# Modulation units placed singly, two groups of them behind the second norm, values turned two units later, and the residual loaded in four parts

## The reference

```python
mod = silu(c) @ w_ada + b_ada                    # 2048 x 12288, one row
sh1, sc1, g1, sh2, sc2, g2 = split(mod, 6)
h = rms_norm(x, g) * (1 + sc1) + sh1
u, q, k, v, ga, gb = split(h @ w_in)             # ga, gb: 2048 wide, the others 1024
y_ssm = s5_branch(u)                             # scan, gelu, then y * sigmoid(y @ w_glu)
y_att = attention(q, k, v)                       # 8 heads of 128
merged = sigmoid(ga) * (y_ssm @ w_proj_ssm) + sigmoid(gb) * (y_att @ w_proj_attn)
x = x + g1 * (merged @ w_out)
h2 = rms_norm(x, g') * (1 + sc2) + sh2           # the second norm
x = x + g2 * (square(relu(h2 @ w_ff1)) @ w_ff2)
x = rms_norm(x, g'')
# the second block: conv and gated recurrence, 32-head windowed attention, w_out_2, MLP; it is not touched
```

## Time and profile before

| | us |
|---|---|
| median of 3 runs | 3233.09 (3228.68 to 3240.85) |
| the profiled execution, its own time | 3230.05 |
| its span, first to last instruction | 3228.7 |
| PE busy in it | 3064.6 (95%) |
| DVE busy | 2135.8 (66%) |
| ACT busy | 1376.7 (43%) |
| mean granted clock of PE | 0.979 of full speed |

### The profile page before, as it was taken

The page is one execution under the profiler, slowest core; times in us unless marked ns, Lnnn a source line. Parts: engine busy times, 40 slices in busy tenths (PEclk is TensorE's granted clock), DMA queues, the critical chain, the costliest instruction groups (busy, mean ns, idle before and its releaser), DMA issues.

```text
span 3228.7 us, 48855 instructions
## 1 busy us (share of the span) xinstructions
PE 3064.6 (95%) x20283; PEld 2762.3 (86%) x20283; DVE 2135.8 (66%) x2568; ACT 1376.7 (43%) x1682; POOL 307.3 (10%) x255
## 2 busy tenths in 40 slices
PE   5799988998899999999998999999999999999998
PEld 1588878898888888888998999999999888888887
DVE  6689996677777554655787776666455755555555
ACT  2233323333353443434455564544444544444343
POOL 4547650000000000000000000000000100000000
PEclk8899999999999999999999999999999999999999
DMA  8855558867767666566555555445555556565664
GB/s 302 276 173 164 164 174 276 278 229 254 254 198 271 189 194 191 186 197 188 177 158 170 170 176 164 147 151 161 177 189 170 178 188 186 194 192 191 189 190 155
DMA packets 311483, 632.08 MB, mean 196 GB/s; under 512 B 30096, under 2 KB 34816, under 8 KB 310624
## 3 DMA queue, kind: packets, MB, share of 16 engines
q1 hardware_dynamic: 298496, 618.74, 59.4%
q10 hardware_dynamic: 11904, 5.61, 0.6%
q0 software_dynamic: 864, 4.60, 0.5%
HBM read 624.66 MB, written 4.21 MB: 195 GB/s over the span
## 4 chain that ended last, share of the span: by engine, by line
PE 77%; DVE 11%; DMA 7%; ACT 2%; issue 2%; ACTq 1%; SPq 0%; DVEq 0%
PE PS L918 13%; PE PS L905 12%; PE PS L906 11%; PE PS L907 11%; PE PS L922 7%; PE PS L934 6%; PE PS L936 6%; PE PS L935 6%; DVE wlo L1743 3%; DMA raw<-in_w_in 2%; ACT whi L2257 2%; DVE aacc L1732 2%; DMA raw<-in_w_ada 1%; DMA raw<-in_w_proj_attn 1%; DMA raw<-in_w_out 1%
## 5 line engine op out<-in xcount | busy, mean ns | idle before, releaser
L1743 DVE TENSOR_TENSOR wlo<-raw,whi 128x1024 fp32r<-128x1024 f32 x983 | 1244.4, 1270 | 920.9 <-ACT whi L2257 919.5
L2257 ACT ACTIVATE whi<-raw 128x1024 fp32r<-128x1024 f32 x983 | 1036.0, 1058 | 1386.7 <-PE PS L907 503.6
L905 PE MATMUL PS<-R,whi 128*128 128x256 f32 x4160 | 1209.5, 291 | 57.0 <-DVE wlo L1743 38.2
L906 PE MATMUL PS<-R,whi 128*128 128x256 f32 x4160 | 1189.4, 286 | 0.0
L907 PE MATMUL PS<-R,wlo 128*128 128x256 f32 x4160 | 1189.0, 286 | 0.0
L905 PEld LDWEIGHTS PS<-R,whi 128*128 128x128 f32 x4160 | 810.5, 195 | 99.4 <-issue 47.0
L906 PEld LDWEIGHTS PS<-R,whi 128*128 128x128 f32 x4160 | 811.0, 195 | 0.8 <-issue 0.7
L907 PEld LDWEIGHTS PS<-R,wlo 128*128 128x128 f32 x4160 | 810.2, 195 | 0.0
L918 PE MATMUL PS<-R,whi 128*128 128x512 f32 x1920 | 484.7, 395 | 14.7 <-DVE R L1660 8.6
L918 PEld LDWEIGHTS PS<-R,whi 128*128 128x128 f32 x1920 | 348.0, 190 | 78.6 <-issue 15.4
L934 PE MATMUL PS<-whi,R 128*128 128x512 f32 x896 | 350.1, 391 | 1.6 <-issue 0.9
(11 more groups left out here) (356 smaller groups left out, 1833.8 us busy)
## 6 DMA issues: line engine op xcount, KB each, us to landing
raw<-in_w_in SPq DMA_DIRECT2D x295, 512.0 KB, 4.1
raw<-in_w_ff SPq DMA_DIRECT2D x256, 512.0 KB, 4.0
raw<-in_w_ada SPq DMA_DIRECT2D x175, 512.0 KB, 4.8
raw<-in_w_mlp_up SPq DMA_DIRECT2D x128, 512.0 KB, 4.1
raw<-in_w_mlp_down SPq DMA_DIRECT2D x128, 512.0 KB, 3.9
raw<-in_w_out SPq DMA_DIRECT2D x64, 512.0 KB, 4.3
raw<-in_w_rnn_proj SPq DMA_DIRECT2D x32, 512.0 KB, 3.6
raw<-in_w_attn_proj SPq DMA_DIRECT2D x32, 512.0 KB, 3.7
```

The source lines that it names most:

```text
L905: pe.matmul(o, whi[:, s, c:c + P], x.operand.hi(k), start=first, stop=False, skip_group_check=True)
L906: pe.matmul(o, whi[:, s, c:c + P], x.operand.lo(k), start=False, stop=False, skip_group_check=True)
L1743: v.tensor_tensor(wlo[:, i % SPN, :], words(j), whi[:, i % SPN, :].bitcast(F32), ALU.subtract).then_inc(lo_done, 1)
L2257: a.activation(whi[:, i % SPN, :], words(j), ACT.Copy).then_inc(hi_done, 1)
```

## The change

- The planner's table gets other points, and at most one modulation unit follows a weight unit (two where four or more are late), where the old loop placed all that were late. By the new table groups 8 and 9 lie mostly behind unit 210 and end at unit 300.
- `turn_v` starts two units after the end of the v panel on PE; ACT's `turned_v` lets three turns pass first.
- The residual comes in four transfers of 512 KB, each with its own semaphore: quarter 0 after four heads and unit 137 (`unit_done` 138), quarter 2 after unit 145, quarter 1 after eight heads and unit 155, quarter 3 after unit 165. `rope_loads` stand behind them on POOL. DVE's residual of panel p waits for quarter p.
- `norm2` is started one unit earlier on ACT and DVE, ahead of the preparation of unit 203.

```diff
-ADAP = ((8, 0), (78, 16), (128, 62), (193, 107), (207, 107), (236, 128))
+ADAP = ((8, 0), (78, 16), (185, 96), (207, 96), (300, 128))
...
-        while extra and n >= resume and 128 - len(extra) < int(np.interp(n, xs_, ys_)):
+        late = int(np.interp(n, xs_, ys_)) - 128 + len(extra)
+        for e in range(min(1 if late < 4 else 2, late) if n >= resume else 0):
             units.append(extra.pop(0))
             if len(extra) % 16 == 0:
                 closes.append(close_at(n - LOOK + 1 + LAG))
                 resume = closes[-1][0] + LOOK + 1
+                break
...
-            if n in (end_of["v", 0], end_of["v", 1]):
-                new.append(turn_v(0 if n == end_of["v", 0] else 1))
+            for i in range(2):
+                if n == end_of["v", i] + 2:
+                    new.append(turn_v(i))
...
             if done is evac_v["res1"]:
-                v.wait_ge(x2_in, 16)
+                v.wait_ge(x2_in[p], 16)
...
-            if n == end_of["w_out", 3] + 1:
+            if n == end_of["w_out", 3]:
                 new.append(norm2())
...
         def turned_v(g):
+            for i in range(3):
+                yield
             for i in range(2):
                 a.wait_ge(v_turned, 2 * g + i + 1)
...
         def second_loads():
-            g.wait_ge(ya_ready, 8)
+
             g.wait_ge(x_saved, 16)
-            g.dma_start(fv(XR, 4096), scr_x).then_inc(x2_in, 16)
+            for p, heads, n in ((0, 4, 138), (2, 4, 146), (1, 8, 156), (3, 8, 166)):
+                g.wait_ge(ya_ready, heads)
+                g.wait_ge(unit_done, n)
+                g.dma_start(fv(XR + 1024 * p, 1024), scr_x[:, 1024 * p:1024 * p + 1024]).then_inc(x2_in[p], 16)
```

More of the change, by code:

```diff
@@ L300, in program @@
     acc_done, row_done = sem("acc_done"), sem("row_done")
-    c_in, small_in, x_in, hot_in, bc_in, bias_in, x2_in, rope_in = (sem(n) for n in (
-        "c_in", "small_in", "x_in", "hot_in", "bc_in", "bias_in", "x2_in", "rope_in"))
+    c_in, small_in, x_in, hot_in, bc_in, bias_in, rope_in = (sem(n) for n in (
+        "c_in", "small_in", "x_in", "hot_in", "bc_in", "bias_in", "rope_in"))
+    x2_in = [sem(f"x2_in{p}") for p in range(4)]
     x_saved, bias_saved, out_saved = sem("x_saved"), sem("bias_saved"), sem("out_saved")
@@ L2507, in side @@
                 bias_loads()
-            if n == end_of["pa", 3]:
+            if n == end_of["v", 1]:
                 second_loads()
```

## The result

The changed kernel took 3208.31 us (median of 4 runs, 3205.73 to 3209.66) against 3232.86 us of the kernel before beside it: 24.6 us less by the medians. The ratio over the runs is 0.9913, 95% interval 0.9899 to 0.9927, which is 24 to 33 us less. The forecast was 3189, in a range of 3170 to 3215: the direction and the range hold, the gain by the medians is a little over half of the 42.5 us of the sum, and 3208 lies nearer to the two rivals at 3211 and 3212 than to the forecast.

A forecast was written before the change was run, and what follows sets the result against it. PE, busy 95% of the span, bounds the kernel; only its idle and slow-clock time, mostly from late weight feed between 459 and 1031 us, can go. Terms sum to 42.5 us: 3230.05 − 42.5 = 3187.5, for a median 3189; range 3170 to 3215.

The forecast's parts named there:

- the two rivals at 3211 and 3212: 3211: only the three single waits count, 21.5 us, chance 0.12; 3212: units 152 to 186 at 2.3 us a unit, 0.14.
- the waits for `wlo` before 640 us: Sign of being right: PE's waits for these weights before 640 us come to under 4 us in all.
- the feed waits in units 152 to 186: Sign of being right: PE waits 10 to 20 us for weights in these units, more than before the change.
- nothing new is late: Units 104 to 127: turning v two units later removes waits of 6.45 and 4.8 us and delays nothing else.
- Bank 7 is used by nobody else meanwhile: At the later turn of v: no other work needs this PSUM bank, so the delay adds no wait.
- 4.5 us given: Units 138 to 151: loading the residual in quarters removes the 5.3 us wait around unit 152; saved 4.5.
- 0.8 us given to the norm: Units 187 to 199: starting the second norm earlier saves 0.8 us, within bounds of 0 to 1.2.
- units 84 to 103, 20 given: Weight feed without bursts of modulation units, at 1.8 us a unit, saves 20 us, or 13 at 2.0.
- the dense stretch, −4.6 given: Units 152 to 186: 64.7 units at 1.94 us each take 125.5 us, 4.6 lost; bounds 4.4 won, 8.5 lost.
- the rival's 2.3: Units 152 to 186: at 2.3 us a unit they take 149 us, 23 worse than the sum, total 3212; chance 0.14.
- behind unit 208, 4.4 given: Units 208 to 239: 4.35 us of PE idle time goes; with about 1 lost later, 3.4 saved.
- The two closes are moved, not changed: From 931 us: closes of two modulation groups come later, after unit 255, at unchanged cost.

The follow-up runs named there:

- e2: Changed kernel with the values turned at once, as before the change: 3206.11 us, ratio 0.9922 to the kernel before.
- e12: Changed kernel with a flatter planner table, ACT's panel-end rounding and squares and DVE's dependent steps one unit later, and values turned at once: 3188.94 us, ratio 0.9867.
- e1: Changed kernel with the old planner (old table, old loop), the other three parts kept: 3227.01 us, ratio 0.9987 to the kernel before.
- e3: Changed kernel with the residual loaded whole once the eighth head is done: 3213.18 us, ratio 0.9940 to the kernel before.
- e4: Changed kernel with norm2 started at unit 200 again: 3207.73 us, ratio 0.9923 to the kernel before.
- e5: Changed kernel loading 256 KB in place of 512 for each modulation unit of groups 2 to 9: 3207.07 us, ratio 0.9910 to the kernel before.
- e7: Changed kernel with DVE accumulating only 64 of 1024 columns of each modulation unit of groups 2 to 9: 3197.22 us, ratio 0.9878 to the kernel before.
- e6: Changed kernel with ACT's panel-end rounding and squares, and DVE's steps behind them, one unit later: 3193.26 us, ratio 0.9870 to the kernel before.
- e8: Changed kernel with a flatter planner table, fewer modulation units behind units 168 to 186: 3201.45 us, ratio 0.9894 to the kernel before.

## Why the prediction was right, and where it was off

**Right: what binds, and the direction.** PE's idle time in units 84 to 239 fell from 62.1 us of 572.4 to 41.5 of 538.8, the clock rose to 0.98 to 1.00 up to the glu, no wait for L1938 is left, none of 5 us at unit 152, and both closes stand behind unit 255. In five of the nine stretches of the table the term is within 1.1 us, in part by luck: with 1.7 us taken out for each close that moved, which is an estimate, it would be two of the nine. Two signs of being right failed: the waits for `wlo` before 640 us were 5.2 us and not under 4, and the feed waits in units 152 to 186 were 22.4 us and not 10 to 20. The last step of the sum has a slip as well: 3187.5 + 3 is 3190.5, not 3189.

**Right, with the wrong owner: the turn.** The prediction gave the later turn the 11.2 us of its waits and said "nothing new is late". e2, e12 and e1 show that it is worth nothing by itself: without bursts ACT is not late and the wait at once is 1.1 us at each panel end, given back by the heads; with bursts the wait goes to the copy that holds bank 7, and to the group's close behind unit 131. "Bank 7 is used by nobody else meanwhile" was false for the old placement, in which a close on that bank falls at unit 131. The sum was not hurt, since the planner removed the same waits; that this term came out is luck.

**Right: the residual and the norm.** 4.5 us given, 4.4 in its stretch (e3), 4.9 by the medians. 0.8 us given to the norm, 0.8 in the wait (e4). The page of the Trainium skill that speaks for transfers of 1 MiB or more (DMA: Bandwidth & Descriptors, section Bandwidth) did not decide here: four of 512 KB were 5 us better than one of 2 MB. Their own rate was not the reason: 2 MB landed in 10.6 us in e3, 512 KB in 4.2 to 8.2. The weight loads issued within a few us of the whole one landed 11.8 to 13.1 us after their issue in e3 (medians by weight), those near quarter 2 after 5.5 to 7.1 in the changed kernel. e3 undoes the size and the spacing in time together, so which of the two helps is not shown.

**Off: units 84 to 103, 20 given, 13.7 measured.** The term set 38 units x 1.8 = 68.4 us against 67.2 us of own work over the whole stretch. The time is lost inside it. In the changed kernel units 88 to 96 are fed late and units 97 to 103 have time over:

```profile
481.38:517.07 35.69, 30.13 (x222) 28.12 (x221) 25.12 (x23) 9.91 (x11) 8.28 (x12) 0.95 0.90 299
517.07:542.50 25.43, 25.43 (x193) 23.51 (x193) 17.54 (x18) 12.43 (x15) 0.00 (x0) 1.00 0.87 287
```

The first has 20 weight and modulation units and the bias loads, 22 in 35.7 us, 1.6 us each, faster than assumed, and PE still stands 5.6 us. The engines prepare at most three units ahead, so spare time of one stretch can't pay for another. That this is the reason was read from the two stretches, and no run tries a greater lead.

**Off: the dense stretch, −4.6 given, −14.1 measured.** This is the step that failed: "I take 1.94", a mean pace carried over from the kernel before, between bounds of 1.8 and 2.0. Measured 2.09, beyond them, though the rival's 2.3 was not reached. A mean pace does not carry over to another placement there: e1, with the old placement and the quarters and rope loads in the stretch, has 62.7 units in 121.8 us, 1.94 each, just the pace that was taken; with two modulation units more in all, and three more in units 168 to 186, it is 134.9. e5 and e7 show that neither bytes nor DVE's time set it. e6 shows that the order at six panel ends (a seventh, which it moves too, lies at unit 191) makes up 14.6 us; that a panel end costs the more the less lead there is fits e1 and e8, but more slots or a greater lead were not tried. The rival's sentence "each panel end there stops ACT and DVE" had the mechanism, with a chance of 0.14. It also fits e8: 3.7 us for a modulation unit in this stretch.

**Off the other way: behind unit 208, 4.4 given, 10.0 measured**, because only idle time was counted; 95.8 us were busy in the earlier trace rows and 90.2 are now. Of the 5.6 us, 3.4 are two closes that moved behind; the other 2.2 are short gaps between matmuls that count as busy. Behind unit 240 the stretch is 3.6 us longer, and 3.4 of it are these two closes: the 21 moved units cost 0.2 us there, not 1. "The two closes are moved, not changed" was right, but the terms are by stretch.

## What to carry to other kernels

When many small jobs share a ring of buffers with the critical stream, count them against the time in each short stretch that the ring's depth can level out (here three units), not over the whole phase: 27 small jobs in place of 25 looked harmless in units 152 to 186, but three more of them in units 168 to 186 went with 11.8 us more. A burst's cost shows up at whatever stands in order behind it, so a fix at that place (the later turn) may be worth nothing once the burst is gone, and may only move the wait while it is there. Before pricing a crowded stretch by a pace, look for an engine that waits in its program order with a landed buffer behind it: moving that wait by one unit gave 14.6 us in units 152 to 186, where half of the bytes of the modulation units gave at most 4.6.

## What the runs showed of the hardware

A transfer of 256 KB landed 4.7 us after its issue where 512 KB took 5.3, in the same stretch, and the 512 KB transfers beside it in the same kernel 4.7 to 5.1: with three or four of them under way, halving the bytes of one took at most 0.6 us off. And units 0 to 15 took 79.5 to 85.6 us in the profiles of kernels that are the same up to there; with what lies ahead of unit 0, unit 84 began at 459 to 469 us. That shifts all that follows by up to 10 us, so single executions can't tell changes of less by their total. Stretches between units do better, but not all alike: units 104 to 119 vary by 4 us, units 208 to 239 not at all. The windows view from 0 to 120 us gives PE's clock as 0.83 before and 0.86 after, and 0.73 to 0.86 over all the profiles; the changed kernel and e4 have the same 0.86 there, with 85.6 and 79.8 us for units 0 to 15, so the clock alone does not explain the spread, and the cause was not tried.
